# Expert weights of a decoder trunk: the first quad's transfers in order of use, and the second quad's loads moved into the loop

## The reference

```python
for l in range(DEPTH):
    mix = hybrid_mixer(x, w_in[l], w_ret_o[l], w_dsa_o[l], w_out[l])
    h = layer_norm(DEEPNORM_ALPHA * x + mix, ln1_g[l], ln1_b[l])
    ffn = hierarchical_moe(h, ...)      # top-1 group of 4, top-2 of its 8 experts, per token
    x = layer_norm(DEEPNORM_ALPHA * h + ffn, ln2_g[l], ln2_b[l])
...
    return (jax.nn.silu(xb @ w_gate[e]) * (xb @ w_up[e])) @ w_down[e]   # one expert
```

## Time and profile before

| what | value |
|---|---|
| median of 3 runs | 1703.43 us (1703.03 to 1705.89) |
| the profiled execution | 1703.03 us, its span 1701.2 us |
| TensorE busy | 1392.0 us (82%), mean granted clock 0.899 |
| VectorE / ScalarE busy | 619.6 us (36%) / 380.6 us (22%) |
| moved by the DMA engines | 527.62 MB, mean 310 GB/s; SP's queue takes 77.2% of the 16 engines' span |

### The profile page before, as it was taken

The page is one execution under the profiler, slowest core; times in us unless marked ns, Lnnn a source line. Parts: engine busy times, 40 slices in busy tenths (PEclk is TensorE's granted clock), DMA queues, the critical chain, the costliest instruction groups (busy, mean ns, idle before and its releaser), DMA issues. The chain is left out here.

```text
span 1701.2 us, 21959 instructions
## 1 busy us (share of the span) xinstructions
PE 1392.0 (82%) x8566; PEld 948.3 (56%) x8566; DVE 619.6 (36%) x1082; ACT 380.6 (22%) x430; POOL 0.2 (0%) x4
## 2 busy tenths in 40 slices
PE   4999999999767757767779999999997567766756
PEld 3998789986313313322369987899843133323313
DVE  2788667554000000000257885865520000000003
ACT  2333644322000000000133346343210010000000
POOL 0000000000000000000000000000000000000000
PEclk8999999999888778867979999999998788788878
DMA  5555435589999999999924553365999999999994
GB/s 194 192 192 204 143 126 208 202 347 403 415 420 416 416 419 418 416 418 420 380 77 171 197 199 112 138 251 188 407 386 415 418 419 416 417 421 416 416 420 173
DMA packets 132406, 527.62 MB, mean 310 GB/s; under 512 B 7536, under 2 KB 11888, under 8 KB 99440
## 3 DMA queue, kind: packets, MB, share of 16 engines
q1 hardware_dynamic: 130192, 519.66, 77.2%
q10 hardware_dynamic: 2144, 6.99, 1.1%
HBM read 525.58 MB, written 1.05 MB: 310 GB/s over the span
## 5 line engine op out<-in xcount | busy, mean ns | idle before, releaser
L758 PE MATMUL psum<-ring,aqT 128*32 128x512 f32 x1984 | 343.1, 839 | 240.3 <-PEq L750 240.3
L758 PEld LDWEIGHTS psum<-ring,aqT 128*32 128x32 f32 x1984 | 90.3, 147 | 484.4 <-issue 484.4
L1276 DVE TENSOR_TENSOR w_low<-ring,w_high 128x2048 fp32r<-128x2048 f32 (+2 forms) x112 | 248.8, 2261 | 108.4 <-DVEq L1275 106.3
L925 ACT ACTIVATE w_high<-ring 128x2048 fp32r<-128x2048 f32 (+2 forms) x112 | 206.0, 1888 | 210.1 <-ACTq L922 201.9
L492 PE MATMUL psum<-w_high,x_high 128*128 128x512 f32 (+2 forms) x384 | 152.3, 396 | 24.3 <-PEq L472 24.3
L1491 DVE TENSOR_TENSOR qk<-psum,qk 128x512 f32<-128x512 f32 x16 | 11.1, 692 | 419.7 <-DVEq L1490 419.7
L492 PE MATMUL psum<-w_high,x_low 128*128 128x512 f32 (+2 forms) x384 | 150.3, 391 | 0.0
L492 PE MATMUL psum<-w_low,x_high 128*128 128x512 f32 (+2 forms) x384 | 149.6, 390 | 0.0
L724 PEld LDWEIGHTS psum<-aqT,h 128*128 128x128 f32 x576 | 138.7, 334 | 17.1 <-issue 17.1
L512 PE MATMUL psum<-x_high,w_high 128*128 128x256 f32 x512 | 146.8, 287 | 0.0
L724 PE MATMUL psum<-aqT,h 128*128 128x128 f32 x576 | 142.6, 408 | 2.2 <-PEq L625 1.6
(11 more groups left out here) (214 smaller groups left out, 1615.4 us busy)
## 6 DMA issues: line engine op xcount, KB each, us to landing
ring<-in_w_up_dram SPq DMA_DIRECT2D x126, 1024.0 KB, 19.5
ring<-in_w_gate_dram SPq DMA_DIRECT2D x122, 1024.0 KB, 16.6
ring<-in_w_down_dram SPq DMA_DIRECT2D x112, 1024.0 KB, 18.3
ring<-in_w_in_dram SPq DMA_DIRECT2D x36, 2048.0 KB, 8.1
ring<-in_w_ret_o_dram SPq DMA_DIRECT2D x8, 2048.0 KB, 8.7
ring<-in_w_dsa_o_dram SPq DMA_DIRECT2D x4, 2048.0 KB, 8.5
ring<-in_w_out_dram SPq DMA_DIRECT2D x4, 2048.0 KB, 7.7
spare<-in_w_gate_dram SPq DMA_DIRECT2D x4, 1024.0 KB, 10.7
```

The lines of the kernel that those rows point to most:

```text
L758: mm = nc.tensor.matmul(bank[s, :], lhs[:, c, s], w[:, k, n * NB:(n + 1) * NB], start=(c == 0), stop=(c == chunks - 1))
L925: nc.scalar.activation(half_tile(high, to, w, b), half_tile(ring, i % RAW, w, b), ACT.Copy).then_inc(high_ready, 1)
L1276: V.tensor_tensor(half_tile(low, i % RAW, w, b), half_tile(ring, i % RAW, w, b), half_tile(high, of, w, b).bitcast(f32), ALU.subtract).the ...
```

## The change

Two things on SP's queue; no engine's arithmetic and no other wait is touched.

In `EARLY` and `FIRST` the places and events stay as they were and in the same order, for the first 21 of the 24 units, but the units put there now follow the order of use: units 14 to 18 go early, then 0 to 13, then 19 and 20. Units 21 to 23 no longer go to `spare0`, `spare1` and `rv1` (these hold 14, 15 and 16 from the mixer on); 21 and 22 go to ring places 8 and 9 once half 0 is used, and 23 to ring place 10 once half 2 is used, a wait that was not there before.

The written-out loads of the second quad go. One wait, for `half_used[1]`, remains of them, and the loop begins with quad 1. So the second quad's half n now waits for what the loop's waits name: its halves 0, 1 and 2 for halves 3, 4 and 5 of the first quad, its halves 3 to 5 for its own halves 0 to 2. Before, its halves 0, 1 and 2 waited for halves 1, 2 and 3 of the first quad, and its half 3 for 4, 5 and its own half 0.

```diff
-EARLY = [(0, "spare0", "rg0"), (1, "spare1", "rg0"), (2, "rv1", "dsa0"), (15, "rg0", "out1"),
-         (16, "qk0", "out1")]
-FIRST = [(3, 2, "mid"), (4, 3, ""), (11, 8, ""), (12, 9, ""), (17, "rg1", ""), (7, 4, "out00"),
-         (8, 6, ""), (18, "rv0", "rv"), (5, 0, "out10"), (13, 10, ""), (9, 5, "out01"), (10, 7, ""),
-         (6, 1, "out11"), (14, 11, ""), (19, "x1", "x1"), (20, "x0", "x0"), (21, "spare0", "half0"),
-         (22, "spare1", ""), (23, "rv1", "")]
+EARLY = [(14, "spare0", "rg0"), (15, "spare1", "rg0"), (16, "rv1", "dsa0"), (17, "rg0", "out1"),
+         (18, "qk0", "out1")]
+FIRST = [(0, 2, "mid"), (1, 3, ""), (2, 8, ""), (3, 9, ""), (4, "rg1", ""), (5, 4, "out00"),
+         (6, 6, ""), (7, "rv0", "rv"), (8, 0, "out10"), (9, 10, ""), (10, 5, "out01"), (11, 7, ""),
+         (12, 1, "out11"), (13, 11, ""), (19, "x1", "x1"), (20, "x0", "x0"), (21, 8, "half0"),
+         (22, 9, ""), (23, 10, "half2")]
...
-                             half0=half_used[0],
+                             half0=half_used[0], half2=half_used[2],
...
-                for u in range(6 * QUAD):
-                    if u % QUAD == 0:
-                        n = (1, 2, 3, 0, 1, 2)[u // QUAD]
-                        if u == 3 * QUAD:
-                            sp.wait_ge(half_used[4], 1).then_inc(half_used[4], -1)
-                            sp.wait_ge(half_used[5], 1).then_inc(half_used[5], -1)
-                        sp.wait_ge(half_used[n], 1).then_inc(half_used[n], -1)
-                    load(l * NE + QUAD, u, later_quad, later_in)
+                sp.wait_ge(half_used[1], 1).then_inc(half_used[1], -1)
                 sp.wait_ge(npass_sp, 1).then_inc(npass_sp, -1)
                 passes = sp.value_load(npass[0:1, 0:1], min_val=1, max_val=SEQ // SLOTS)
-                with sp.Fori(2, passes * QUADS) as q:
+                with sp.Fori(1, passes * QUADS) as q:
```

## The result

The changed kernel takes 1715.74 us (median of four, 1715.06 to 1717.76) against 1703.62 us for the kernel before: 1.0076 of its time, 95% interval 1.0062 to 1.0089. It is slower by 12.1 us; 1716.0 was forecast, within 1707.5 to 1722.6. Ten executions of it are on record in all, 1715.03 to 1719.17 us with a median of 1716.5. Its profiled execution took 1715.03 us, span 1713.2 us.

The account below looks back on a forecast made before the run. The prediction took the expert stages to be bound by DMA, so a dry queue is lost time. Holes of 6.5 us in each layer, 13.0 in all, added to the profiled 1703.0 gave 1716.0 us, range 1707.5 to 1722.6.

Parts of the forecast that it names:

- What bounds the kernel: Expert stages: end when their bytes land plus a fixed PE chain; a hole in the DMA queue is lost for good.
- the prediction's sum: Both layers' turns from mixer to experts: holes of 6.5 us each, 13.0 us in all.
- The order of the first 21 units: First quad's loads: same places and events, nothing read comes later; cost and gain 0.
- faster: Turn into the experts: halves come free sooner and the turn's own hole closes, 5 us gained, 1698; chance 0.03.
- Unit 23's wait and the second quad's loads: DMA queue at the turn: later issues leave first-layer holes of 1.8, 1.05 and 3.65 us.
- The restart: Dry DMA queue at the turn: rate counts as full 1.7 us after a load's issue.
- The lower one: Holes at the turns: if the slowest DMA engine sets PE's wait, 2.2 us a layer less, 4.5 in all.
- The upper bound: Restarts at the turns: 1.1 us more at each of six stops, 19.6 us in all.
- PE's clock, the rival with 0.07: First quad: halves at the low clock lengthen the holes by 3 us each, two a layer, 1728; chance 0.07.
- The slower stream, a unit in 2.9 us, the rival with 0.02: Expert loads at the turn: a slower stream shrinks holes to 3.5 us a layer, 1710; chance 0.02.
- The loop's entry: SP's queue after unit 23's issue: entry hidden before the next wait ends, 0; uncovered up to 1.5 us a layer.

Follow-up runs that it names:

- run 3: Changed kernel with the second quad written out and its units 0 to 7 all waiting for half 4: 1737.66 us, ratio 1.0198.
- run 2: Changed kernel with the second quad written out and its units 4 to 7 issued right behind units 0 to 3, at half 3: 1709.92 us, ratio 1.0039.
- run 1: Kernel before, first quad's order and places kept, only the second quad's loads moved into the loop: 1716.73 us, ratio 1.0080.
- run 6: Changed kernel with the second quad's loads written out instead of looped, each behind the same half: 1717.13 us, ratio 1.0084.
- run 4: Kernel before with later waits for the second quad's units 4 to 15, not later than the queue lasts: 1703.50 us, ratio 1.0001.
- run 5: Kernel before with the first rows of units 21 to 23 issued halfway through gate half 0: 1701.69 us over 12 runs, ratio 0.9991.
- run 9: The kernel of run 5, unchanged, profiled again; gate half 0 at the low clock in both layers: 1702.91 us.

## Why the prediction was right, step by step

**What bounds the kernel.** Shown: 16.5 us of holes a layer, as reckoned, cost 34.2 us in all (run 3), 2.85 a layer cost 6.5 (run 2), 6.5 a layer cost 12 to 14 (the changed kernel, runs 1 and 6), and a delay of 13.9 us without a hole costs nothing (run 4). These are four points on one line, and the prediction's sum was one of them.

**The number.** That 1715.74 lies 0.3 us from 1716.0 is in part luck. The ten executions spread over 4 us, and their median, 1716.5, is 13.1 us over the 1703.4 of the kernel before. The mechanism gave 13.4 us in the profiled pair, of which PE's clock in one late half gave 1.5 back; no term of the sum had that.

**The order of the first 21 units: 0.** Run 1 against the changed kernel (1.0080 and 1.0076) leaves room for no more than about 2 us either way, the width of their intervals. The rival that had the new order free halves sooner ("faster") falls too: halves 2, 3 and 4 came free 0.2 us later, and the turn's own hole stays (123 GB/s from 400 to 402, before 143).

**Unit 23's wait and the second quad's loads: holes of 1.8, 1.05 and 3.65 us.** They measured 1.8, 1.2 and 3.8, and 1.9, 1.3 and 3.6. Run 1 adds what the prediction did not say: as long as the queue is dry when half 4 comes free, it does not matter how the idle time before is divided. The loss is then fixed by the last restart (half 4 at 423.5) less the work issued before it: seven units in the changed kernel, 17.5 us of the 24 between the first restart at 401.4 and the last at 425.4. Where 11 units are issued before it the last hole is gone; run 4, which issues them early enough, has none at all, and run 2, whose last eight go only from 410, keeps the first two.

**The restart, 1.7 us after an issue.** In the first layer the queue is full up to 422, and 422 to 427 lost 3.8 us, as if it were full again from 425.8. That is 2 us after the issue; so 1.7 was a little short, and the holes with it: 6.8 for 6.5.

**The bounds.** The lower one assumed that the slowest DMA engine's lag pays for a part of every hole. Of 6.8 us a layer by bytes, 7.0 and 6.4 arrived at the last quad; that is the whole within the 0.6 us by which profiles of the kernel before differ there, where this bound has 2.2. The upper bound's 1.1 us a stop, 19.6 in all, did not appear either: with these waits the largest loss measured is 13.7 (run 6).

**PE's clock, the rival with 0.07.** It did not decide here, but it is real, at another place than it was put: in the changed kernel's stretches around the holes the granted clock is 1.00, while half 0 does not always run at it. There it costs 2.2 to 2.4 us each, since the queue is dry behind it. The rival's 3 us was the price of a half that is low nearly throughout (6.45 against 3.5); half 0 only begins low and took 5.5 us against 3.6. The kernel before has this exposure as well, so the difference between the two kernels hardly carries it.

**The slower stream, a unit in 2.9 us, the rival with 0.02.** The changed kernel moves 418 GB/s outside the holes, and the holes are 6.8 us a layer where this rival had 3.5.

**The loop's entry: 0.** Shown by run 6 (1.0084 for 1.0076, intervals overlapping).

Open: why half 0 starts at the low level in some executions and not in others. Its work and the work ahead of it are the same; no run here varied them. The traces narrow it down. In the first layer of all twelve profiled executions the granted clock falls to 0.50 around the two gathers of tokens ahead of half 0, and what differs is when. In the kernel before it is low from about 388 to 395, and half 0 begins at 395.8, at the high level; in run 1 it is low from 393.7 to 400.4, and half 0 begins at 396.7, inside it. The three executions with this half 0 low (runs 1, 2 and 9) are also the three that begin the first gather last, at 387.03 to 387.16 us, against 386.04 to 386.76 in the nine others. That is a coincidence in time and not a cause shown.

## What to carry to other kernels

In a stage that is bound by DMA, write down the queue as a timeline of its own: what is issued, when it can be, and how long it carries. In these runs a wait cost the time for which the queue was dry because of it, to within about 1.2 us in all, and a new order that left every load's time of issue as it was cost nothing above 2 us. One written-out turn between two loops may be worth its lines (here 12 us), because it is the place where the consumer frees places in another rhythm. And where the queue is dry, the consumer's clock is on the path, even in a kernel where a slower consumer is otherwise hidden.

## What was not expected of the hardware

The clock of TensorE in gate half 0 differs from execution to execution of one kernel, and moves the total by 2.2 to 2.4 us a layer. The three profiled executions of run 5's kernel (1698.28 to 1702.91) cover nearly the whole spread of its single runs (1697.78 to 1703.09), so it may explain most of that; for the runs without a profile this is not shown. It makes a change of 0.1% hard to see. The mean clock of the whole span does not tell it: of the twelve runs the five slowest have means of 0.906 and 0.907, and the two fastest 0.898 and 0.901.
